# More quadrants of a convolution and MLP layer are transposed by transfers instead of by TensorE

## The reference

```python
h = rmsnorm(x, mix_norm)
b_gate, c_gate, v = split(h @ w_in, 3)          # w_in: 2048 x 6144
u = c_gate * v
y = causal_depthwise_conv(u, conv_w)            # 3 taps along the tokens
x = x + (b_gate * y) @ w_out                    # 2048 x 2048
a = relu(rmsnorm(x, mlp_norm) @ w1)             # 2048 x 8192
x = x + (a * a) @ w2                            # 8192 x 2048
```

## Time and profile before

| | |
|---|---|
| median of 3 runs | 1902.61 us |
| profiled execution | 1902.01 us, span 1900.2 us |
| PE busy | 1892.1 us |
| PE weight loads busy | 1568.6 us |
| DVE busy | 1678.3 us |
| ACT busy | 1036.5 us |
| DMA | 537.87 MB, mean 283 GB/s |
| granted TensorE clock | 1.00 |

### The profile page before, as it was taken

One profiled execution on the slowest core, in us unless ns is written; L12 is line 12 of the kernel. 1 busy time (PEld: TensorE's weight loads), 2 busy tenths in 40 slices (PEclk: granted clock), 3 DMA queues, 4 the chain that ended last, 5 costly groups with the idle time before them and its releaser, 6 DMA issues.

```text
span 1900.2 us, 22331 instructions
## 1 busy us (share of the span) xinstructions
PE 1892.1 (100%) x8540; PEld 1568.6 (83%) x8540; DVE 1678.3 (88%) x1500; ACT 1036.5 (55%) x1110; POOL 150.9 (8%) x242
## 2 busy tenths in 40 slices
PE   9999999999999999999999999999999999999999
PEld 8888888888888888888888888888888888888887
DVE  6689899898999898989989899898998889788878
ACT  6464564545558477586675866745444343334432
POOL 0100010000011111120110201100000000000000
PEclk9999999999999999999999999999999999999999
DMA  9774768749676976987968879699988878877783
GB/s 372 263 261 124 265 206 326 234 120 329 216 208 267 354 241 205 338 282 241 357 221 326 288 243 356 222 397 403 357 328 344 346 283 314 352 314 278 294 328 118
DMA packets 137306, 537.87 MB, mean 283 GB/s; under 512 B 27888, under 2 KB 31984, under 8 KB 112240
## 3 DMA queue, kind: packets, MB, share of 16 engines
q1 hardware_dynamic: 103072, 412.65, 56.7%
q0 software_dynamic: 33984, 123.75, 21.3%
q10 hardware_dynamic: 144, 0.04, 0.0%
HBM read 438.35 MB, written 94.37 MB: 280 GB/s over the span
## 4 chain that ended last, share of the span: by engine, by line
PE 68%; DMA 1%; ACT 0%; issue 0%; DVE 0%; SPq 0%; ACTq 0%
PE pair L1293 66%; PE pair L1328 1%; DMA raw<-in_turns 1%; SPq L410 0%; DVE raw L985 0%; ACT sum L695 0%; ACT quads L749 0%; DVE sum_l_mix L1022 0%; ACT ring L651 0%; ACT junk L759 0%; ACT quads L701 0%; DVE x L1100 0%; ACT act L769 0%; ACTq L650 0%; ACTq L360 0%
## 5 line engine op out<-in xcount | busy, mean ns | idle before, releaser
L1293 PE MATMUL pair<-ring,act 128*128 128x512 f32 x7728 | 1767.0, 390 | 1.5 <-issue 1.2
L1293 PEld LDWEIGHTS pair<-ring,act 128*128 128x128 f32 x7728 | 1446.2, 188 | 302.5 <-issue 4.1
L651 ACT ACTIVATE ring<-raw 128x1024 fp32r<-128x1024 f32 x659 | 696.4, 1060 | 798.3 <-PE pair L1293 512.1
L991 DVE TENSOR_TENSOR ring<-raw,ring 128x1024 fp32r<-128x1024 f32 x659 | 792.2, 1221 | 159.1 <-ACT ring L651 156.8
L985 DVE TENSOR_TENSOR raw<-raw 128x1024 f32<-128x1024 f32 x312 | 367.8, 1220 | 9.9 <-DMA raw<-in_turns 1.7
L518 POOL DMA_DIRECT2D spill<-stage x136 | 78.6, 617 | 488.2 <-ACT stage L774 372.8
L531 POOL DMA_DIRECT2D raw<-in_turns x56 | 50.4, 1053 | 701.2 <-DVE raw L985 701.2
L972 DVE TENSOR_TENSOR stage<-quads,stage 128x1024 fp32r<-128x1024 f32 x68 | 83.0, 1221 | 23.8 <-ACT stage L774 23.1
L1306 PE MATMUL pair<-ring,act 128*128 128x512 f32 x384 | 87.3, 389 | 0.0
L1306 PEld LDWEIGHTS pair<-ring,act 128*128 128x128 f32 x384 | 72.0, 188 | 14.9
L774 ACT ACTIVATE stage<-quads 128x1024 fp32r<-128x1024 f32 x68 | 71.5, 1051 | 15.9 <-DVE quads L889 6.2
(11 more groups left out here) (107 smaller groups left out, 527.8 us busy)
## 6 DMA issues: line engine op xcount, KB each, us to landing
raw<-in_turns SPq DMA_DIRECT2D x191, 1024.0 KB, 7.5
act<-spill SPq DMA_DIRECT2D x290, 512.0 KB, 6.8
spill<-stage POOLq DMA_DIRECT2D x136, 512.0 KB, 9.3
act<-act_kept SPq DMA_DIRECT2D x74, 512.0 KB, 7.0
raw<-in_turns POOLq DMA_DIRECT2D x56, 512.0 KB, 8.4
act_kept<-act POOLq DMA_DIRECT2D x28, 512.0 KB, 9.6
x_tok<-in_x SPq DMA_DIRECT2D x4, 1024.0 KB, 14.8
x<-mixed SPq DMA_DIRECT2D x8, 512.0 KB, 18.3
```

Source lines behind the costliest of these rows:

```text
L651: nc.scalar.activation(ring[g % RING][:, 0], raw[:, raw_of(v, s), 2 * (s % 2):2 * (s % 2) + 2, :], ACT.Copy).then_inc(hi_ready, 1)
L991: nc.vector.tensor_tensor(ring[g % RING][:, 1], raw[:, raw_of(v, s), 2 * (s % 2):2 * (s % 2) + 2, :], ring[g % RING][:, 0].bitcast(F32), A ...
L1293: mm = nc.tensor.matmul(bank, stationary, moving, start=(opens and k == 0 and n == 0), stop=(closes and k == NT - 1 and n == 2))
```

## The change

Eight quadrants of c times v (two in each of pairs 0, 1, 3, 4) and the first quadrant of the up pairs 8 to 14 now go by planes and a transposing transfer as well; the fourth quadrant of those pairs goes so as before, and the last up pair, 15, keeps PE for all four.

- UP: ACT writes the first quadrant's planes at slot 13 of the odd turn, behind its scaling; SP issues the transfer at the end of its list for that turn, behind the load of R21; ACT joins and squares it at slot 1 of the even turn.
- GATED: ACT writes planes at slots 4 and 6, merges them into `u_pad` at slots 6 (ahead of the second planes) and 8; SP issues both transfers at the start of its list for that turn. These planes lie in the stage buffers.
- PE turns no quadrant in GATED pairs and only the second and third in up pairs 8 to 14; its wait before L12's bank is changed to fit.
- The load of x11 moves from turn 31 to the end of turn 32.

The diff, cut:

```diff
 def by_transfer(q):
 
-    return KINDS[q] == UP and q < NQP - 1
...
-TURNED = [0]
+    return 2 if KINDS[q] == GATED or (KINDS[q] == UP and q < NQP - 1) else 0
+
+
+TURNED, TRANSFERS = [0], [0]
 for _q, _kind in enumerate(KINDS):
-    TURNED.append(TURNED[-1] + (2 if _kind == GATED else 4 - by_transfer(_q)))
+    TURNED.append(TURNED[-1] + (2 if _kind == GATED else 4) - by_transfer(_q))
+    TRANSFERS.append(TRANSFERS[-1] + by_transfer(_q))
...
-        planes = at("planes", ACTS2 + 24 * KB, [P, 2, 2 * BW], U16)
-        planes_t = at("planes_t", ACTS2 + 28 * KB, [P, 4 * NT, P], U16)
+        planes = [at(f"planes{i}", where, [P, 2, 2 * BW], U16) for i, where in enumerate((STAGE + 4 * KB, ACTS2 + 24 * KB))]
+        planes_t = [at(f"planes_t{i}", where, [P, 4 * NT, P], U16) for i, where in enumerate((STAGE + 8 * KB, ACTS2 + 28 * KB))]
...
+        def turned_before(q, m):
+            return m - (1 if by_transfer(q) and m > 0 else 0)
...
+            def turn_planes(q, n):
+                sp.wait_ge(planes_out, 2 * (TRANSFERS[q] + n) + 2)
+                up = KINDS[q] == UP
+                sp.dma_start_transpose(planes_t[up][:], planes[up][:].rearrange("p z e -> p (z e)")).then_inc(planes_in, 16)
...
                 if v % 2 == 0 and v <= V_DOWN and by_transfer(v // 2 - 1):
 
-                    sp.wait_ge(planes_out, 2 * (v // 2 - UP0))
-                    sp.dma_start_transpose(planes_t[:], planes[:].rearrange("p z e -> p (z e)")).then_inc(planes_in, 16)
+                    q = v // 2 - 1
+                    for n in (0, 1) if KINDS[q] == GATED else (1,):
+                        turn_planes(q, n)
...
-                        q, place = {L11: ("11", x11), S1: ("21", x21), L12: ("22", x22), S3: ("12", x12)}[j]
-                        load_mixed(q, place)
+                        if j != L11:
+                            q, place = {S1: ("21", x21), L12: ("22", x22), S3: ("12", x12)}[j]
+                            load_mixed(q, place)
+                    if v == V_DOWN and j == L22:
+                        load_mixed("11", x11)
+                if v % 2 and v < V_DOWN and KINDS[v // 2] == UP and by_transfer(v // 2):
+                    turn_planes(v // 2, 0)
...
 
                 if KINDS[q] == GATED:
                     act.wait_ge(u_formed, FORMED_U[q] + (2, 4, 2, 4)[m])
-                if KINDS[q] != GATED or m in (0, 3):
-                    act.wait_ge(quad_turned, TURNED[q] + ({0: 1, 3: 2}[m] if KINDS[q] == GATED else m + 1))
+                else:
+                    act.wait_ge(quad_turned, TURNED[q] + turned_before(q, m) + 1)
...
-            def put_planes(q):
-
-                act.wait_ge(rectified, RECTIFIED[q] + 8)
-                words = sums_of(q)[5][:].bitcast(U16).rearrange("p t (b c z) -> p z b t c", c=P, z=2)
+            def put_planes(q, m):
+                if KINDS[q] == GATED:
+                    act.wait_ge(u_formed, FORMED_U[q] + 2 * (m + 1))
+                    act.wait_ge(act_formed, 8)
+                    act.wait_ge(act_lo_ready, direct_done(1, S3))
+                    if q > Z0:
+                        for i in (1, 2):
+                            act.wait_ge(spilled[i], 16 * stage_uses(1, i))
+                else:
+                    act.wait_ge(rectified, RECTIFIED[q] + 2 * m + 2)
+                first, _, _, _, _, l22 = sums_of(q)
+                held = first if m == 0 else l22
+                words = held[:].bitcast(U16).rearrange("p t (b c z) -> p z b t c", c=P, z=2)
                 for z in range(2):
-                    nc.scalar.activation(planes[:, z].rearrange("p (b t c) -> p b t c", b=NT, t=2), words[:, z],
-                                         ACT.Copy).then_inc(planes_out, 1)
-
-            def square_planes(q):
-
-                act.wait_ge(planes_in, 16 * (q - UP0 + 1))
+                    nc.scalar.activation(planes[KINDS[q] == UP][:, z].rearrange("p (b t c) -> p b t c", b=NT, t=2),
+                                         words[:, z], ACT.Copy).then_inc(planes_out, 1)
+
+            def turned_words(q, z):
+                return planes_t[KINDS[q] == UP][:, 2 * NT * z:2 * NT * (z + 1)]
+
+            def square_planes(q, m):
+
+                n = m // 3
+                act.wait_ge(planes_in, 16 * (TRANSFERS[q] + n + 1))
                 quads_free(act, q)
-                o = quad["L21"]
+                o = quad[("L11", "L21")[n]]
                 words = o.bitcast(U16).rearrange("p a (t z) -> p z (a t)", z=2)
                 for z in range(2):
-                    nc.scalar.activation(words[:, z], planes_t[:, 2 * NT * z:2 * NT * (z + 1)].rearrange("p a t -> p (a t)"),
+                    nc.scalar.activation(words[:, z], turned_words(q, z).rearrange("p a t -> p (a t)"),
                                          ACT.Copy).then_inc(merged, 1)
-                act.wait_ge(merged, 2 * (q - UP0 + 1))
+                act.wait_ge(merged, 4 * (q - UP0) + 2 * n + 2)
                 o = o.rearrange("p a t -> p (a t)")
                 nc.scalar.activation(o, o, ACT.Square).then_inc(quad_ready, 1)
...
             def take_u(q, half):
-                act.wait_ge(quad_turned, TURNED[q] + half + 1)
+                act.wait_ge(planes_in, 16 * (TRANSFERS[q] + half + 1))
                 act.wait_ge(y_step, 2 * FORMED_U[q])
                 act.wait_ge(pad_ready, 1)
-                o = u_pad[:, :, CW - 1 + HALF * half:CW - 1 + HALF * (half + 1)]
-                nc.scalar.activation(o, by_channels(), ACT.Copy).then_inc(quad_ready, 1)
+                first = 2 * (CW - 1 + HALF * half)
+                words = u_pad[:].bitcast(U16)[:, :, first:first + 2 * HALF].rearrange("p a (t z) -> p z a t", z=2)
+                for z in range(2):
+                    ins = nc.scalar.activation(words[:, z], turned_words(q, z).rearrange("p (a b) t -> p a (b t)", b=2), ACT.Copy)
+                ins.then_inc(quad_ready, 1)
...
                             copy_first(q)
                         if s == 13 and KINDS[q] in (GATE, UP):
                             scale_tokens(q, 0)
+                            if KINDS[q] == UP and by_transfer(q):
+                                put_planes(q, 0)
                     if 2 <= v <= V_DOWN and v % 2 == 0:
                         kind = KINDS[q - 1]
                         if kind in (GATE, UP) and s in (2, 3, 4):
                             scale_tokens(q - 1, s - 1)
-                        if kind == UP and s in (3, 5, 6):
-                            square_quad(q - 1, {3: 0, 5: 1, 6: 2}[s])
-                        if by_transfer(q - 1) and s == 5:
-                            put_planes(q - 1)
+                        if kind == UP and by_transfer(q - 1) and s == 1:
+                            square_planes(q - 1, 0)
+                        if kind == UP and s == 3 and not by_transfer(q - 1):
+                            square_quad(q - 1, 0)
+                        if kind == UP and s in (5, 6):
+                            square_quad(q - 1, s - 4)
+                        if kind == UP and by_transfer(q - 1) and s == 5:
+                            put_planes(q - 1, 3)
                         if kind == UP and s == 7 and not by_transfer(q - 1):
                             square_quad(q - 1, 3)
-                        if by_transfer(q - 1) and s == 8:
-                            square_planes(q - 1)
+                        if kind == UP and by_transfer(q - 1) and s == 8:
+                            square_planes(q - 1, 3)
                         if kind == GATED and s in (6, 8):
                             take_u(q - 1, s // 2 - 3)
+                        if kind == GATED and s in (4, 6):
+                            put_planes(q - 1, s // 2 - 2)
                         if kind == GATED and s in (9, 10, 11, 12):
                             first_tap(q - 1, s - 9)
...
-                o = (first, l22)[m] if kind == GATED else (first, s1, s4, l22)[m]
-                if kind == GATED:
-                    pe.wait_ge(u_formed, FORMED_U[q] + 2 * (m + 1))
-                elif kind == MIXED:
+                o = (first, s1, s4, l22)[m]
+                if kind == MIXED:
                     pe.wait_ge(added, pair_added(q) + FINISHED[m])
                 else:
                     pe.wait_ge(rectified, RECTIFIED[q] + 2 * m + 2)
-                if q == 0 and m == 0:
-                    pe.wait_ge(plain_copied, 4)
-                if m > 0:
+                if m > by_transfer(q) // 2:
                     pe.wait_ge(quad_ready, TURNS[q] + m)
...
-                        pe.wait_ge(quad_ready, TURNS[v // 2] - by_transfer(v // 2 - 1))
+                        if v == PLAIN_TURNS:
+                            pe.wait_ge(plain_copied, 4)
+                        elif KINDS[v // 2 - 1] == GATED:
+                            pe.wait_ge(added, pair_added(v // 2 - 1) + 6)
+                        else:
+                            pe.wait_ge(quad_ready, TURNS[v // 2] - by_transfer(v // 2 - 1) // 2)
...
```

(7 more changed lines are left out.)

## The result

The changed kernel takes **1947.18 us** (median of 4, 1943.0 to 1949.13) against 1902.65 (4) of the kernel before beside it: ratio **1.0228**, 95% interval 1.0208 to 1.0248, so about 44 us slower. Forecast was 1922 with a range of 1904 to 1930: right in sign, under half of the size (+19.6 against +44.5), and out of the range. The profiled execution is the fastest of the four (1943.0, span 1941.3), 41.1 us over the span of before.

A forecast was written before the change was run, and what follows sets the result against it. PE was taken as the bound, with a chain through ACT and DVE 1.6 us behind. 1902.0 + 16.1 (up pairs) + 5.8 (gated pairs) - 1.7 (x11, turn 32) = 1922.2, predicted 1922 us, range 1904 to 1930.

The forecast's parts named there:

- PE stops being the only bound in up turns: Up pairs: a loop through DVE, load, transfer, join and ACT takes 81.2 us against 78.88, +2.3 a pair.
- PE is then no part of the loop.: Up pairs, transfer behind the load: the loop runs through DVE from slot 9 to slot 13, taken as 44.7 us.
- The transfer waits for R21's load and lands 1.9 us behind it.: Up pairs, SP's queue: load issued at 1115.6 takes 4.7 us, transfer 1.9 more, landing at 1122.2 instead of 1121.0.
- Rival (1): Up pairs: R21's load doesn't hold up the transfer, as the engines may interleave the two; 1906 us, chance 0.13.
- Split of slot 2 late, slot 4 late, no pause behind it.: ACT in up pairs: split of slot 2 comes 1.6 to 2.8 us late, and the delay reaches slot 9 unabsorbed.
- margin as at slot 9: Up pairs: DVE's low half of slot 9 ends 1.6 us before PE wants it.
- Turn 4, 8 and 10 stop at slot 7.: Gated turns 4, 8, 10: PE idles 2.8 us at slot 7, as its split stands behind transfer, merge and second planes.
- x11: Turn 32: moving x11's 1 MB load out of the full queue removes PE's wait for a square, -1.7 us.
- The load and the transfer 6.6.: Up pairs, term of the loop: R21's load 4.7 us plus the transfer's 1.9 behind it.
- Rival (3): Transfers also meet spills and accumulating loads, each landing some 0.5 us later, 15 x 0.5; 1929 us, chance 0.09.
- +5.8: Four gated pairs: turns 4, 8 and 10 cost 2.3 us each, turn 2 gains 1.1; bounds -6.9 and +9.
- With the transfer alone: 0.0 a pair.: Up pairs, transfer not behind the load: PE waits 0.9 us against 0.86 saved, so 7 x 0.0 = 0.

The follow-up runs named there:

- the kernel with the idle quadrant: The changed kernel, with PE still turning the first quadrant of the seven up pairs, which nobody reads: 1948.88 us, ratio 1.0233.
- the filler kernel: The kernel with the gated part alone (1915.74 us), plus 11 unread small matmuls ahead of slot 6 in turns 4, 8 and 10: 1913.88 us.

## Why the prediction was wrong

Most of its mechanism held, but not its picture of the loop, and the terms of the sum were too small. Step by step:
- **PE stops being the only bound in up turns; a loop with the transfer in it sets the period.** Right: the kernel with the idle quadrant gives PE 7.2 us of work back at no cost, and putting the transfer ahead of the load takes 23.2 us off.
- **"PE is then no part of the loop."** Wrong. The split of slot 13 waits 1.66 us for PE in the change, as it did before, and PE is busy without a pause for the 57.09 us ahead of it. The forecast went through DVE from slot 9 to slot 13 instead (44.7). DVE's low half of slot 13 waits only 0.19 us for that split (902.01 in the change), so the two ways are equally long to 0.2 us, and that the number came out all the same is luck. What it hid is that a slower PE lengthens the period, which is where the clock comes in.
- **The transfer waits for R21's load and lands 1.9 us behind it.** Right (1.9 in the pair shown, 1.6 where the load took 7.7, 1.8 to 1.9 in four others, 3.2 in the first). Rival (1), the two interleaved, is out. The Trainium skill (DMA: Bandwidth & Descriptors, Queues, rings and completion order) says that each DMA engine takes a queue's descriptors in the order of the ring; the trace agrees, with landings of 5.0 to 8.9 us behind the load and 3.6 to 3.7 in six of seven cases ahead of it, but it can't tell that order from SP being held up in its issue, which shows the same landings.
- **Split of slot 2 late, slot 4 late, no pause behind it.** Right: 6.77 us from the one to the other. PE's wait showed up one step earlier than forecast, at the read of the second quadrant ahead of slot 4 and not at the ring's slot 8 or 9. The same place in the trace of before, ACT and then PE:

```profile
1133.91 1.01 ACT L701 ACTIVATE quads<-pair 128x1024 f32<-128x1024 f32 x1
```

```profile
1136.52 1.03 PE L1328 MATMUL pair<-eye,sum 128*128 128x128 f32 x8
```

The read ended at 1134.92, 1.6 us ahead of PE: the same margin as at slot 9, and I had looked only at slot 9. With equal margins it changes nothing in the sum.
- **Turn 4, 8 and 10 stop at slot 7.** Right: 3.04, 3.02 and 3.15 us against 2.8.
- **x11:** right.

The rest of what failed are sizes. The sum fell short of the profiled execution by 20.9 us, 12.2 in the up pairs and 8.7 in the gated ones:
1. **"The load and the transfer 6.6."** It was 7.8 in the mean (7.0 to 9.3). The 4.7 of the load was one row, the least of its kind: in six pairs of the kernel before, the load of this place took 4.7 to 5.1, and in the change 5.1 to 7.7. 7 x 1.2 = 8.4 us of the 12.2 by which the up pairs were short. Why the load takes longer in the change stays open. In the pair with 7.7 it isn't POOL's loads: POOL issues them at 1159.41, behind both landings (1157.1 and 1158.7). Rival (3), transfers half a microsecond late, had the direction and less than half the size.
2. **The granted clock had no term.** Behind PE's pause it read 0.50 for up to 3 us in five of the seven pairs: at 926.04 and 1008.11 as the windows show, and at 843.68, 1174.26 and 1256.56, where the eight transposes took 1.36 to 1.85 us instead of 1.06. About 0.9 us in each of the two pairs worked out above, and what is left of the 12.2 for all seven is 3.8. In the gated turns it is the 1.9 that the filler kernel gave back, if that is more than noise.
3. **The gated pairs, "+5.8".** Short by 8.7 us. By the pauses that PE's rows list, 0.3 for each restart, and what the slow matmuls take over 0.2271 each: turn 2 pauses 1.23, 0.61 and 0.27, so 2.1 + 0.9 - 1.7 saved = +1.3 (forecast -1.1); turn 4 3.6 + 0.9 + 1.6 of slow work - 1.7 = +4.4 (forecast 2.3); turns 8 and 10 pause 1.25, 3.02, 0.20 and 3.15, so 7.6 + 1.2 + 3.2 of slow work - 3.4 saved - 0.6 for the pause that turn 8 had before, and 0.6 for one of 0.42 in turn 7 that the kernel before lacks and that I can't explain = +8.6 (forecast 4.6). Sum 14.3 of 14.5. In turn 2 most of the miss is the landing, 5.3 us where I took 3.7 (the other first landings were 4.3 and 4.4). The pause of 1.25 stands at the start of turn 8, where it was 0.33: the quadrant taken from its place had hidden DVE's T2, so its 0.86 was no saving. The slow work, 4.8 in all, stands partly in place of the waits at slot 8 that the forecast had at 0.8 each; the filler kernel gives back 1.9 of it. The 7 restarts of turns 4, 8 and 10 and 3 of turn 2 were in no term.
4. **"With the transfer alone: 0.0 a pair."** The forecast's own sum for the loop, with 5.4 for the transfer alone in place of 6.6, gives 80.0, and the kernel with the transfer ahead has 79.9 (near, with the same luck: there too the split of slot 13 waits for PE). I had used the loop's sum for the one case and the first pair's margin for the other. Rival (1) should have been 1902.0 + 7 x 1.1 + 5.8 - 1.7 = 1914, and the lower end of the range with it.

What the profiled execution does not hold is that the four runs of the change spread over 6.1 us. The landings vary from pair to pair by up to 3.9 us on the path, which can do that; it was not tried.

## What to carry to other kernels

When PE is 100% busy and a chain lies 1.6 us behind it, work taken off PE is worth at most the margin, and a wait put into the chain costs its full length in every turn: write down the period of each loop, with the same terms for every case, before counting what leaves the bound engine. A transfer on which an engine waits goes ahead of bulk loads on its queue; here the order alone was worth 23 us. Trace the loop step by step through the engine that seems to be off it: here ACT's split of slot 13 still waited for PE in every pair, and so the clock counted. Take a load's time as a range and not from its quickest row: the load that took 4.7 to 5.1 us before took 5.1 to 7.7 in the change.

## What the runs showed of the hardware

- SP needs longer to issue a transposing transfer behind a load that is still under way: 3.0 to 5.6 us, against 1.6 ahead of it (2.9 once). From the end of the issue to the landing it is 2.0 to 2.1 us in six of the seven pairs of the change (3.4 in the first) and in the pairs of the kernel with the transfer ahead.
- A transposing transfer between other places of SBUF took longer: 4.3 us or more in the gated turns of the change, with slices near 215 GB/s in turn 4 (186.1 to 190.5), against 3.6 and slices near 290.
- The granted clock fell to half behind pauses of PE of 2.43 us (at 1008.11) and held behind one of 2.50 (1008.85 in the kernel with the idle quadrant), and behind one of 2.72 in the change itself (1090.41, transposes of 1.06 us), so the length of a pause alone did not decide it. The Trainium skill (TensorE: Matmul & The Clock Gate, HAM oscillation — how this bites in real kernels) has pauses between bursts of matmuls as what brings the lower clock back; the trace agrees that pauses do it, with 0.50 in the windows above.
- A slow stretch of 3 us need not cost its 1.5: where PE will wait for the ring next, slower matmuls only fill that wait (turn 4: 7.7 us with either clock).
